# Up projection by seven products: weight casts on ScalarE, weight sums on GpSimd, and the last blocks' activations split earlier

## The reference, cut to what matters

```python
def conv_gated_mlp(n, w_up, conv_w, conv_b, w_down):
    u = n @ w_up                       # 1024 x 1024 @ 1024 x 5632
    u = causal_conv3(u, conv_w) + conv_b
    gate, val = u[..., :D_FF], u[..., D_FF:]      # D_FF = 2816
    return (jax.nn.silu(gate) * val) @ w_down
```

## Time and profile before

| | |
|---|---|
| median of 3 runs | 2933.8 us (2929.73 to 2936.27) |
| profiled execution | 2931.2 us |
| its span | 2929.1 us |
| busy: TensorE, VectorE, ScalarE, GpSimd | 2794.4, 1685.7, 957.9, 1049.7 us |
| granted TensorE clock, mean | 0.981 |

### The profile page before, as it was taken

The page is one execution under the profiler, slowest core; times in us unless marked ns, Lnnn a source line. Parts: engine busy times, 40 slices in busy tenths (PEclk is TensorE's granted clock), DMA queues, the critical chain, the costliest instruction groups (busy, mean ns, idle before and its releaser), DMA issues.

```text
span 2929.1 us, 36991 instructions
## 1 busy us (share of the span) xinstructions
PE 2794.4 (95%) x13264; PEld 2208.1 (75%) x13264; DVE 1685.7 (58%) x1938; ACT 957.9 (33%) x1580; POOL 1049.7 (36%) x698
## 2 busy tenths in 40 slices
PE   6999999999999999998999989999999999999998
PEld 5888886766677777677777777888788777777776
DVE  6554466544544335468887875554136666477764
ACT  4322326655600003243232230102124444254441
POOL 5311303333333331117999982321220010321125
PEclk8999999999999999999999999999999999999999
DMA  5200100000111110122222242221210001000023
GB/s 187 96 28 22 44 7 17 22 22 20 72 47 47 43 45 29 36 72 80 72 79 86 72 150 101 87 94 37 88 43 23 16 16 26 12 7 7 15 108 115
DMA packets 174988, 160.17 MB, mean 55 GB/s; under 512 B 20225, under 2 KB 151009, under 8 KB 174609
## 3 DMA queue, kind: packets, MB, share of 16 engines
q1 hardware_dynamic: 173456, 150.01, 16.2%
q10 hardware_dynamic: 1408, 8.50, 0.8%
HBM read 129.93 MB, written 28.38 MB: 54 GB/s over the span
## 4 chain that ended last, share of the span: by engine, by line
PE 73%; issue 8%; DVE 8%; POOL 7%; ACT 3%; DMA 1%; POOLq 0%; SPq 0%; ACTq 0%; DVEq 0%
PE ps L788 16%; PE ps L789 16%; PE ps L790 16%; POOL w_high L1267 3%; POOL up_weights L1267 2%; PE ps L3131 2%; PE ps L2971 2%; PE ps L2803 2%; PE ps L2795 2%; PE ps L697 1%; PE ps L2726 1%; PE ps L2696 1%; PE ps L3026 1%; PE ps L2934 1%; PE ps L3227 1%
## 5 line engine op out<-in xcount | busy, mean ns | idle before, releaser
L1204 POOL CAST w_high<-w_raw 128x1024 fp32r<-128x1024 f32 x153 | 168.2, 1099 | 1624.8 <-PE ps L790 998.6
L788 PE MATMUL ps<-NH,w_high 128*128 128x512 f32 (+1 forms) x1288 | 496.1, 385 | 10.3 <-DVEq L1958 4.8
L789 PE MATMUL ps<-NL,w_high 128*128 128x512 f32 (+1 forms) x1288 | 495.5, 385 | 0.0
L790 PE MATMUL ps<-NH,w_low 128*128 128x512 f32 (+1 forms) x1288 | 493.2, 383 | 0.0
L1206 POOL TENSOR_TENSOR w_low<-w_raw,w_high 128x1024 fp32r<-128x1024 f32 x153 | 389.5, 2546 | 12.2
L895 DVE TENSOR_TENSOR hT<-hT,ps 128x1024 f32<-128x1024 f32 x168 | 205.0, 1221 | 208.3 <-PE ps L790 208.3
L788 PEld LDWEIGHTS ps<-NH,w_high 128*128 128x128 f32 x1288 | 244.6, 190 | 63.6 <-issue 8.1
L790 PEld LDWEIGHTS ps<-NH,w_low 128*128 128x128 f32 x1288 | 244.8, 190 | 46.8
L789 PEld LDWEIGHTS ps<-NL,w_high 128*128 128x128 f32 x1288 | 243.9, 189 | 47.7 <-issue 0.9
L788 PE MATMUL ps<-act_high,w_high 128*128 128x512 f32 x352 | 140.4, 399 | 13.5 <-issue 7.7
L790 PE MATMUL ps<-act_high,w_low 128*128 128x512 f32 x352 | 140.2, 398 | 0.0
(11 more groups left out here) (455 smaller groups left out, 6551.8 us busy)
## 6 DMA issues: line engine op xcount, KB each, us to landing
w_raw<-in_w_in SPq DMA_DIRECT2D x69, 512.0 KB, 3.8
w_raw<-in_w_out SPq DMA_DIRECT2D x24, 512.0 KB, 3.5
w_raw<-in_w_up SPq DMA_DIRECT2D x24, 512.0 KB, 4.3
act_spill<-conv_val SPq DMA_DIRECT2D x22, 512.0 KB, 2.7
w_raw<-in_w_down SPq DMA_DIRECT2D x22, 512.0 KB, 3.7
act_in<-act_spill SPq DMA_DIRECT2D x22, 512.0 KB, 5.1
up_raw<-in_w_up SPq DMA_DIRECT2D x20, 512.0 KB, 5.0
w_raw<-in_w_xkv SPq DMA_DIRECT2D x8, 512.0 KB, 5.7
```

What stands on the lines that cost most here:

```text
L788: nc.tensor.matmul(o, wh, xh, start=start, stop=False)
L789: nc.tensor.matmul(o, wh, xl, start=False, stop=False)
L790: return nc.tensor.matmul(o, wl, xh, start=False, stop=stop)
L1204: nc.gpsimd.tensor_copy(WH[slot][:, :], w_raw[slot][:, :]).then_inc(w_high, 1)
```

## The change

ScalarE takes over the seven casts of a block (`weight_high`), placed in `up_act` for the next block: cast 0 behind copy 0, cast 1 behind silu, cast 2 behind copy 2, casts 3 and 4 behind copy 3, cast 5 behind conv gate, cast 6 behind copy 6. The four sums move from VectorE's queue to GpSimd's, in front of the block's seven subtractions. Block 0's casts and the start of the fourth plain tile (`first_start(1, 1)`) are written into the first block. In block 19 ScalarE runs `act_high(0)` behind copy 3, and VectorE `act_low(0)` behind addition 5. `act_low(1)` is split in halves behind additions 2 and 4 of update 0, and the later ones in halves behind additions 0 and 2. TensorE's order in tiles 0 and 1 changes for the last two chunks: both of tile 0, then both of tile 1.

```diff
+            def weight_sums(i, par):
+                f1, f2 = raws[par]
+                w11, w12, w21, w22 = (t_[:, k:k + HALF] for t_ in (f1, f2) for k in (0, HALF))
+                s1, s3, s2, s4 = (wS[k][:, :] for k in (0, 1, 2, 3))
+                pool.wait_ge(fw_landed[par], i * 32 + (LOADED + 32))
+                pool.wait_ge(fw_ready, i * 14 + (SB_DONE + 7 * par))
+                pool.wait_ge(t_lo, SB_DONE + 3)
+                nc.gpsimd.tensor_tensor(s1, w21, w22, ALU.add).then_inc(s_sum, 1)
+                nc.gpsimd.tensor_tensor(s3, w11, w21, ALU.subtract).then_inc(s_sum, 1)
+                pool.wait_ge(s_sum, i * 8 + (SB_DONE + 4 * par + 1))
+                nc.gpsimd.tensor_tensor(s2, s1, w11, ALU.subtract).then_inc(s_sum, 1)
+                pool.wait_ge(s_sum, i * 8 + (SB_DONE + 4 * par + 3))
+                nc.gpsimd.tensor_tensor(s4, w12, s2, ALU.subtract).then_inc(s_sum, 1)
...
             def up_split(i, par):
-                for k, src in enumerate(sources):
-                    nc.gpsimd.tensor_copy(high, src).then_inc(fw_high, 1)
+                weight_sums(i, par)
+                for k, src in enumerate(weights_of(par)):
                     pool.wait_ge(fw_high, i * 14 + (SB_DONE + 7 * par + k + 1))
                     nc.gpsimd.tensor_tensor(low, src, high.bitcast(F32), ALU.subtract).then_inc(fw_ready, 1)
...
+            def weight_high(i, par, k):
+                act.wait_ge(f_p, i * 14 + (SB_DONE - 7 + 7 * par + k + 1))
+                if k == 0:
+                    act.wait_ge(fw_landed[par], i * 32 + (LOADED + 32))
+                if k in (2, 5):
+                    act.wait_ge(s_sum, i * 8 + (SB_DONE + 4 * par + (3 if k == 2 else 4)))
+                nc.scalar.activation(ring[k][0], weights_of(par)[k], ACT.Copy).then_inc(fw_high, 1)
...
                 up_copy(i, par, 0, gate[:, 0:HALF], Yb)
+                if first:
+                    weight_high(0, 0, 3)
+                    first_start(1, 1)
+                    act.wait_ge(t_lo, SB_DONE + 4)
+                    for k in range(4, 7):
+                        weight_high(0, 0, k)
+                next_high(0)
                 silu(i + par, 1 - par)
+                next_high(1)
                 up_copy(i, par, 2, gate[:, HALF:], Yb)
+                next_high(2)
                 up_copy(i, par, 3, val[:, HALF:], Zb)
+                next_high(3, 4)
+                if last:
+                    act_high(0)
...
                 conv_start(i + 1, par, 0)
+                next_high(5)
                 up_copy(i, par, 6, val[:, 0:HALF], Yb)
+                next_high(6)
...
                 product(i + par, 1 - par)
-                if not last:
-                    weight_sums(i + par, 1 - par)
                 up_add(i, par, 4, val[:, HALF:], Yb, 3)
                 up_add(i, par, 5, gate[:, HALF:], Zb, 2)
                 if behind:
                     behind()
                 taps(i + 1, par, 0)
...
-            up_dve(last, 1, last=True)
+            up_dve(last, 1, behind=lambda: act_low(0))
             taps(UPS // 2, 1, 1)
+            lows = [{0: lambda: product(UPS // 2, 1), 2: lambda: act_low(1, (0,)), 4: lambda: act_low(1, (1,))}]
+            lows += [{0: lambda n=n: act_low(n + 1, (0,)), 2: lambda n=n: act_low(n + 1, (1,))} for n in range(1, DOWNS)] + [{}]
...
+            order = [(c, k) for c in range(C - 2) for k in range(2)] + [(c, k) for k in range(2) for c in range(C - 2, C)]
+            for c, k in order:
```

More of the change, by code:

```diff
@@ L896, in add_update @@
                     .then_inc(job_free[st.slot(k0 + f)], 1)
-                if f == 0 and behind_first:
-                    behind_first()
+                if f in behind:
+                    behind[f]()
                 if norm and f - 1 in ADDS[norm]:
@@ L1575, in act_high, with up_act, next_high @@
                     nc.scalar.activation(aH[n % 2][:, x, :], aF[n % 2][:, x, :], ACT.Copy).then_inc(f_hi, 1)
[L1577 removed]
+            def weight_high(i, par, k):
[4 more added lines that the diff above has]
+                    act.wait_ge(s_sum, i * 8 + (SB_DONE + 4 * par + (3 if k == 2 else 4)))
+                act.nop(nofuse=True)
+                nc.scalar.activation(ring[k][0], weights_of(par)[k], ACT.Copy).then_inc(fw_high, 1)
+            def up_act(i, par, first=False, last=False):
                 gate, val = up[2 * par], up[2 * par + 1]
+                def next_high(*ks):
+                    for k in () if last else ks:
+                        weight_high(i + par, 1 - par, k)
                 act.wait_ge(f_tap, i * 4 + (2 * par + 2))
                 up_copy(i, par, 0, gate[:, 0:HALF], Yb)
+                if first:
[5 more added lines that the diff above has]
+                next_high(0)
                 silu(i + par, 1 - par)
+                next_high(1)
                 up_copy(i, par, 2, gate[:, HALF:], Yb)
+                next_high(2)
                 up_copy(i, par, 3, val[:, HALF:], Zb)
[L1585 to L1586 removed]
+                next_high(3, 4)
+                if last:
+                    act_high(0)
                 act.wait_ge(f_x, i * 6 + (SB_DONE - 6 + 3 * par + 9))
@@ L1602, in _ @@
             first_start(1, 0)
-            first_start(1, 1)
+            for k in range(2):
+                weight_high(0, 0, k)
             act.wait_ge(tile_done, F0.tile(0, 4))
             sum_high(3)
-            with act.Fori(0, UPS // 2) as i:
+            weight_high(0, 0, 2)
+            up_act(0, 0, first=True)
+            up_act(0, 1)
+            with act.Fori(1, UPS // 2 - 1) as i:
                 for par in range(2):
                     up_act(i, par)
+            up_act(UPS // 2 - 1, 0)
+            up_act(UPS // 2 - 1, 1, last=True)
             silu(UPS // 2, 1)
-            for n in range(DOWNS + 1):
+            for n in range(1, DOWNS + 1):
                 act_high(n)
@@ L2197, in up_add, with up_dve @@
                 nc.vector.tensor_tensor(dst, dst, src[par], ALU.add).then_inc(f_x, 1)
-            def up_dve(i, par, last=False, behind=None):
+            def up_dve(i, par, behind=None):
                 gate, val = up[2 * par], up[2 * par + 1]
@@ L2213, in up_dve, with act_low @@
                 taps(i + 1, par, 0)
-            def act_low(n):
-                for x in range(2):
+            def act_low(n, halves=(0, 1)):
+                for x in halves:
                     dve.wait_ge(f_hi, 2 * n + x + 1)
@@ L2234, in _ @@
             up_dve(last, 0)
-            up_dve(last, 1, last=True)
+            up_dve(last, 1, behind=lambda: act_low(0))
             taps(UPS // 2, 1, 1)
-            def last_product():
-                product(UPS // 2, 1)
+            lows = [{0: lambda: product(UPS // 2, 1), 2: lambda: act_low(1, (0,)), 4: lambda: act_low(1, (1,))}]
+            lows += [{0: lambda n=n: act_low(n + 1, (0,)), 2: lambda n=n: act_low(n + 1, (1,))} for n in range(1, DOWNS)] + [{}]
             for n in range(DOWNS + 1):
[L2242 to L2247, removed]
+                add_update(dve, DN if n < DOWNS else F1, n // 2 if n < DOWNS else 0, 8 * (n % 2), lows[n])
             for k in range(6, 8):
@@ L2900, in _ @@
                 wait_pair(pe, F0, 0, k)
-            for c in range(C):
+            order = [(c, k) for c in range(C - 2) for k in range(2)] + [(c, k) for k in range(2) for c in range(C - 2, C)]
+            for c, k in order:
                 pe.wait_ge(n_lo, NORM["ffn"][2] + c + 1)
[L2903 to L2907, removed]
+                for half in range(2):
+                    mm = plain(k, half, c)
+                if c == C - 1:
+                    mm.then_inc(tile_done, 1)
             for k in range(2, 4):
```

36 lines of the change are left out of this document (6 added, 30 removed).

## The result

The changed kernel takes 2903.4 us (median of 4, 2902.6 to 2904.3); the kernel before, on the same chip, 2934.2 (4 runs, 2929.7 to 2936.3). The ratio is 0.9897, 95% interval 0.988 to 0.9914. The profiled execution has 2903.9 us, its span 2901.8, against 2931.2 and 2929.1: 27.3 us less by the spans.

A forecast was written before the change was run, and what follows sets the result against it. GpSimd, through VectorE's sums and addition to P6, was taken to set the 19.97 us block. Gains of 12.0 + 0.5 + 16.5 = 29.0 us took the median from 2933.8 to 2904.8, range 2898 to 2918.

The forecast's parts named there:

- (b): Prologue and block 0: tile 2 gains 2.3 us, P5's 5.1 us wait replaces P6's 3.3; net gain 0.5 us.
- (c): Behind block 19: waits of 7.66 and 5.80 us and slow matmuls mostly go, third job loses 0.9; gain 16.5 us.
- (a): Steady blocks, casts to ScalarE and sums to GpSimd: GpSimd needs 19.0, TensorE paces at 19.3; gain 12.0 us.
- rival 1: Steady blocks: GpSimd stays the bound at 19.6 to 20.5 us each, steady part +6.7 to -9.5; chance 0.20.
- Rival 2: Steady blocks: GpSimd's sums cost 2.09 each by themselves, GpSimd needs 22.2 us, kernel slower at 2957; chance 0.04.
- the end of rival 1: Steady blocks: GpSimd and VectorE overlap nothing, 20.5 us per block, 2926.3 us; chance 0.03 within the 0.20.
- Rival 3: Block 19's end: `act_in`, wanted earlier, lands late; only about 6 of the 16.5 us come, 2915; chance 0.08.
- (d): Later updates: `act_low(n + 1)` halves at additions 0 and 2 remove nothing, as TensorE has no wait there.

The follow-up runs named there:

- the kernel with one more addition: Changed kernel with the fourth weight sum computed once more on GpSimd in every block, cast 5 waiting for it: 2924.0 us, ratio 0.997.
- the kernel without that wait: Changed kernel with ScalarE's cast 2 behind copy 3 instead of in front, in every block: 2900.0 us, ratio 0.9894.
- both orders changed: Changed kernel with cast 2 behind copy 3 and the first product's copy ahead of the third activation-sum cast on ScalarE: 2897.7 us, ratio 0.9879.
- the kernel with two more additions: Changed kernel with the fourth weight sum computed twice more on GpSimd in every block, cast 5 waiting for the last: 2950.1 us, ratio 1.0059.

## Why the prediction held, step by step

The time (2904.8 forecast, 2903.4 measured) and the mechanism held. The table above has the terms. That the medians agree to 1.4 us is in part luck: by the landmarks the sum was 1.7 us too good (29.0 against 27.3), with (b) 2.8 too good and (c) 0.8 too small, and the runs of the kernel before alone are spread over 6.6 us.

*(a) Steady blocks*: forecast 19.3 by TensorE's pace, GpSimd's need 19.0, measured 19.33 and, by the kernel with one more addition, 18.9. The forecast's margin of 0.3 was no wider than its model's error of 0.3 for the kernel before; the measured one is 0.45 us a block. So rival 1 (GpSimd stays the bound) was close, and its chance of 0.20 was fair. Slack of P5: 1.3 forecast, 1.0 measured. The price of a sum on GpSimd, taken as 1.29 between bounds of 1.29 and 2.09, is 1.26 to 1.30 with VectorE idle (block 0 and 1421.81) and 2.06 to 2.28 beside its taps and product. Rival 2 falls: a sum is dear only by the encounter, and the encounters are counted once by VectorE's operations. ScalarE's cast has 0.61 to 0.63, forecast 0.60. The Trainium skill ("ScalarE: Activation LUTs", What ACT_TABLE_LOAD costs) gives 186 ns + 0.833 ns per element for an activation without pointer operands; an estimate from that is 0.61 us for 512, and the trace agrees (0.61 to 0.63).

On the end of rival 1: the Trainium skill ("SBUF — State Buffer", Who interferes with whom) has the second of two such operations wait out the first. By that an encounter with the product (1.22 us alone) would cost GpSimd 1.22; the runs have 0.77 and 0.99. Turn-taking holds, complete exclusion does not.

*(b) Prologue and block 0*: the sum was 2.8 us too good (-0.5 forecast, +2.3 measured), in two terms. First, the gain at tile 2 was 1.5 to 1.6, not 2.3: I followed GpSimd's low part and did not ask what else tile 2 needs. Its PSUM pair is freed by ScalarE's copy, which stood behind a cast waiting for VectorE. With that copy moved ahead tile 2 gains 28.05 - 25.8 = 2.25. Second, for block 0 I had the wait (5.1 forecast, 4.65 measured) but put the lower clock behind it in the range and not in the sum; it was 2.4 us, as the kernel without that wait shows.

*(c) End*: 16.5 forecast; 17.3 in the comparison, 17.2 with the end undone alone. The third job's wait was 0.48 where I had 0.9, and the wait at the second update and the lower clock went. Rival 3 (`act_in` late) did not occur: the first product on `act_high` waits 0.38.

*(d)* The later halves: nothing seen, as forecast; from the second update's third job to the end of the updates, the two kernels keep the same distance.

## What to carry to other kernels

When work is taken off an engine, add up what the relieved engine needs from single operations and from encounters with its neighbour, and set it beside the next engine's pace; idle time in front of an operation is no slack if a neighbour uses it. An operation moved to an engine's queue belongs behind whatever frees a resource there (here copy 3 ahead of cast 2): steady state hid the wrong order with 1.0 us to spare, and the first pass, where nothing has run ahead, paid 6 us for it. A stall of TensorE of over two microseconds is to be costed together with matmuls at half pace that may follow it (here up to 2.4 us).

## What the runs showed of the hardware

*The clock behind a wait.* In all these profiles, TensorE's idle times of 3.76 us (tile 2, both orders changed) to 8.7 us around the blocks were followed by 6 to 13 matmuls at 0.42 to 0.43 us instead of 0.227, at 1.2 GHz instead of 2.4; in block 0 the 7.9 us for 24 matmuls (granted clock 0.65) are 12 at half pace. Shorter ones went either way. The old wait of 3.33 us in block 0 cost nothing more; this is that block in the kernel before (columns as above):

```profile
1347.31:1369.89 22.58, 19.68 (x86) 15.70 (x85) 14.06 (x12) 7.96 (x8) 18.48 (x16) 1.00 0.23 70
```

But of the ten waits of 2.5 us for copy 3 in the kernel with two more additions, six were followed by 7 or 8 matmuls at half pace (P5 and P6 in 6.94 to 6.99 us) and four by none (5.34 to 5.36); where it came, the half pace began only some matmuls after TensorE had resumed. (The 3.33 and the 2.5 are both idle times of the weight loads.) So the length of a wait alone doesn't decide it; what does, these runs leave open.

*Room that isn't there.* Two engines that take turns hide their need: GpSimd was busy 18.2 us of 19.32 and had 0.45 to give, and with one operation more it took two blocks at the old pace before the wait showed.
